# The last experts of a two-block layer: down product of expert 14 moved forward, last up product in staggered column halves, last norm spread over three engines

## The reference, cut to what matters

```python
g, idx = lax.top_k(jnp.swapaxes(aff, 1, 2), cap)        # 16 experts choose 128 tokens each
xs = jax.vmap(lambda hb, ib: hb[ib])(h, idx)
a = jnp.einsum('becd,edf->becf', xs, w_gate)
u = jnp.einsum('becd,edf->becf', xs, w_up)
y = jnp.einsum('becf,efd->becd', jax.nn.silu(a) * u, w_down) * g[..., None]
out = jax.ops.segment_sum(y.reshape(-1, d), flat, num_segments=bsz * n)
...
x = x + gt2 * out
return rmsnorm_2(x, g_final)                            # x * rsqrt(mean(x*x) + eps) * gain
```

## Time and profile before

| what | us |
|---|---|
| median of 3 runs (lowest to highest) | 2581.66 (2574.31 to 2585.56) |
| the profiled execution's own time | 2583.6 |
| its span | 2581.9 |
| PE busy | 2456.7 (95%) |
| DVE busy | 1627.3 (63%) |
| ACT busy | 1058.0 (41%) |
| POOL busy | 211.6 (8%) |

### The profile page before, as it was taken

One profiled execution on the slowest core, in us unless ns is written; L12 is line 12 of the kernel. 1 busy time (PEld: TensorE's weight loads), 2 busy tenths in 40 slices (PEclk: granted clock), 3 DMA queues, 4 the chain that ended last, 5 costly groups with the idle time before them and its releaser, 6 DMA issues.

```text
span 2581.9 us, 30627 instructions
## 1 busy us (share of the span) xinstructions
PE 2456.7 (95%) x11985; PEld 2005.2 (78%) x11985; DVE 1627.3 (63%) x2028; ACT 1058.0 (41%) x1558; POOL 211.6 (8%) x224
## 2 busy tenths in 40 slices
PE   7999889999999999999999999989995999999996
PEld 6787568888888877888787898866684788888884
DVE  6999745225243645444443871477456899999986
ACT  4234434325131221121212522166244677777765
POOL 1000320000000000000000100000103011111100
PEclk9999889999999999999999999999996999999998
DMA  4111021221111322232222311110227899999988
GB/s 149 66 41 45 33 90 68 72 98 34 41 50 44 103 82 99 81 122 81 96 91 71 128 72 34 49 33 18 83 90 269 321 390 391 391 396 392 396 333 298
DMA packets 116412, 370.64 MB, mean 144 GB/s; under 512 B 6309, under 2 KB 15701, under 8 KB 116304
## 3 DMA queue, kind: packets, MB, share of 16 engines
q1 hardware_dynamic: 94832, 293.63, 29.8%
q0 software_dynamic: 21472, 75.51, 9.3%
HBM read 343.89 MB, written 25.26 MB: 143 GB/s over the span
## 4 chain that ended last, share of the span: by engine, by line
PE 83%; DVE 9%; ACT 3%; DMA 2%; issue 2%; POOL 1%; SPq 0%; POOLq 0%; ACTq 0%; DVEq 0%
PE banks L433 24%; PE banks L435 24%; PE banks L434 24%; DVE conv_out L1501 4%; DVE w_lo L427 2%; PE banks L2484 2%; PE banks L533 1%; PE banks L2530 1%; PE banks L2351 1%; PE banks L2330 1%; ACT w_hi L420 1%; DMA expert_w<-in_w_up 1%; PE banks L2499 1%; PE banks L2500 1%; PE banks L2626 1%
## 5 line engine op out<-in xcount | busy, mean ns | idle before, releaser
L2018 DVE TENSOR_TENSOR expert_w_lo<-expert_w,expert_w_hi 128x2048 fp32r<-128x2048 f32 x189 | 427.3, 2286 | 30.3 <-ACT expert_w_hi L1341 28.6
L1341 ACT ACTIVATE expert_w_hi<-expert_w 128x2048 fp32r<-128x2048 f32 x192 | 367.1, 1918 | 153.4 <-PE banks L435 133.1
L433 PE MATMUL banks<-act_hi,w_hi 128*128 128x512 f32 x960 | 376.4, 392 | 7.3 <-DVE w_lo L427 4.1
L434 PE MATMUL banks<-act_lo,w_hi 128*128 128x512 f32 x960 | 374.4, 390 | 0.0
L435 PE MATMUL banks<-act_hi,w_lo 128*128 128x512 f32 x960 | 374.2, 390 | 0.0
L420 ACT ACTIVATE w_hi<-w_raw 128x1024 fp32r<-128x1024 f32 x152 | 156.9, 1060 | 299.1 <-PE banks L435 299.0
L427 DVE TENSOR_TENSOR w_lo<-w_raw,w_hi 128x1024 fp32r<-128x1024 f32 x152 | 181.7, 1223 | 140.4 <-ACT w_hi L420 136.1
L433 PE MATMUL banks<-w_hi,act_hi 128*128 128x512 f32 (+1 forms) x640 | 246.3, 385 | 6.6 <-DVE w_lo L427 3.0
L435 PE MATMUL banks<-w_hi,act_lo 128*128 128x512 f32 (+1 forms) x640 | 243.9, 381 | 0.0
L434 PE MATMUL banks<-w_lo,act_hi 128*128 128x512 f32 (+1 forms) x640 | 243.6, 381 | 0.0
L433 PEld LDWEIGHTS banks<-act_hi,w_hi 128*128 128x128 f32 x960 | 180.7, 188 | 47.9 <-issue 4.2
(11 more groups left out here) (404 smaller groups left out, 4111.1 us busy)
## 6 DMA issues: line engine op xcount, KB each, us to landing
expert_w<-in_w_gate SPq DMA_DIRECT2D x32, 2048.0 KB, 10.8
expert_w<-in_w_up SPq DMA_DIRECT2D x32, 2048.0 KB, 11.1
expert_w<-in_w_down SPq DMA_DIRECT2D x32, 2048.0 KB, 10.8
ada_w<-in_w_ada POOLq DMA_DIRECT2D x48, 512.0 KB, 4.1
w_raw<-in_mlp_up_w SPq DMA_DIRECT2D x16, 1024.0 KB, 5.3
w_raw<-in_mlp_down_w SPq DMA_DIRECT2D x16, 1024.0 KB, 5.0
w_raw<-in_w_in SPq DMA_DIRECT2D x10, 1024.0 KB, 5.3
w_raw<-in_w_in SPq DMA_DIRECT2D x18, 512.0 KB, 6.0
```

The source lines that it names most:

```text
L433: nc.tensor.matmul(o_, lh, rh, start=start, stop=False)
L434: nc.tensor.matmul(o_, lh, rl, start=False, stop=False)
L1341: act.activation(EWH[ring][:, 2 * j:2 * j + 2, :], EW[slot][:, 2 * j:2 * j + 2, :], ACT.Copy).then_inc(w_hi, 1)
L2018: dve.tensor_tensor(EWL[slot][:, c, :], EW[slot][:, c, :], EWH[ring][:, c, :], ALU.subtract).then_inc(w_ready, 1)
```

## The change

- The turn of expert 14 leaves the loop. PE's transposes of expert 14's hidden rows stand in the middle of down 13, and down 14 follows right behind down 13; gate 15 comes after it. Second hidden buffers (`HTH2`, `HTL2`) hold expert 14's.
- Slots: down 14 goes to 2 and 3, up 15 to 4 and 5, down 15 to 2 and 3. Their order in SP's queue is down 14, up 15, down 15, behind gate 15.
- Up 15 runs by pieces in staggered column halves, so that half 0 ends one piece and a half before half 1; the transposes of its first half stand before the last piece of half 1, those of its second half within down 15.
- `expert_y` of expert 14 runs on DVE behind the low part of piece N15+8, and its scatter follows.
- `XB` moves to slots 0 and 1 (also waits for the end of gate 15). ACT copies the gain row to PSUM (`PAIR[2]`). DVE norms tiles 0 to 4 with the gain read from there; POOL multiplies tiles 5, 6 and 7 by gain and then by scale. ACT squares the last rows by halves and scales one half of them, DVE the other.

```diff
         def first_piece(e):
             return 8 + 12 * (e - 1)
...
+        POOL_TILES = (5, 6, 7)
...
             for half in range(2):
-                load_expert(LASTE - 1, 2, half, used=N14 + 8 + 2 * half + 2)
+                load_expert(LASTE - 1, 2, half, used=N14 + 4 + 2 * half + 2, slot=2 + half)
             for half in range(2):
-                load_expert(LASTE, 1, half, used=N14 + 4 + 2 * half + 2)
+                load_expert(LASTE, 1, half, used=N14 + 8 + 2 * half + 2, slot=4 + half)
             for half in range(2):
-                load_expert(LASTE, 2, half, used=N15 + 2 * half + 2, slot=half)
+                load_expert(LASTE, 2, half, used=N15 + 2 * half + 2, slot=2 + half)
+            sp.wait_ge(ex_p, N15 + 8)
             sp.wait_ge(y_out, 16 * (NE - 1))
             for t in range(NT):
                 sp.dma_start(XB[:, t, :], acc_d[tok(t), :]).then_inc(BULK[t], 16)
-            for t in range(NT):
-                sp.wait_ge(pl_x, 8 + t + 1)
+            for t in (0, 1, 2, 3, 5, 4, 6, 7):
+                if t in POOL_TILES:
+                    sp.wait_ge(fp_x, POOL_TILES.index(t) + 1)
+                else:
+                    sp.wait_ge(pl_x, 8 + t + 1)
                 sp.dma_start(out[0, tok(t), :], XB[:, t, :]).then_inc(fin_out, 16)
...
+            pool.wait_ge(w_ready, W_SPLIT + N15 + 16)
...
+            def final_gain(t):
+                pool.tensor_tensor(XB[:, t, :], XB[:, t, :], GF[:, :], ALU.mult).then_inc(fp_g, 1)
...
+            def final_scale(t):
+                pool.wait_ge(fp_g, POOL_TILES.index(t) + 1)
+                pool.wait_ge(fz_scale, TILES_SCALE)
+                pool.tensor_scalar(XB[:, t, :], XB[:, t, :], RS[:, 52 + t:53 + t], None, ALU.mult).then_inc(fp_x, 1)
...
+            pool.wait_ge(pl_sq, 8 + POOL_TILES[0] + 1)
+            final_gain(5)
...
+            for t in POOL_TILES:
+                final_scale(t)
...
@@ ACT @@
+            w_piece_hi(N14 + 11, 5, 1, 0, LASTE - 2)
+            expert_rows_hi(LASTE)
+            w_piece_hi(N15, 2, 0, 1, LASTE)
+            w_piece_hi(N15 + 1, 2, 1, 1, LASTE)
+            expert_hidden_hi(LASTE - 1, HTH2)
+            w_piece_hi(N15 + 2, 3, 0, 2, LASTE)
...
+            w_piece_hi(N15 + 13, 2, 1, 1, NE)
+            act.wait_ge(ex_p, N15 + 8)
+            act.wait_ge(ex_he, LASTE)
+            act.activation(SG[:, :], PAIR[2][:, :], ACT.Silu).then_inc(ex_sg, 1)
             act.activation(SD[:, 63:64], EPSC[:, 0:1], ACT.Sqrt)
...
+            act.activation(PAIR[2][:, :], GF[:, :], ACT.Copy).then_inc(fz_act, 1)
+            w_piece_hi(N15 + 14, 3, 0, 2, NE)
...
+            final_stats(0)
+            w_piece_hi(N15 + 15, 3, 1, 2, NE)
+            final_stats(1)
+            last_hidden_hi(0)
+            final_stats(2)
+            last_hidden_hi(1)
+            for t in range(3, NT):
+                final_stats(t)
+            last_square(0)
+            last_square(1)
...
@@ DVE @@
+            w_piece_lo(N15 + 2, 3, 0, 2)
+            expert_y(LASTE - 1, N14 + 12)
+            w_piece_lo(N15 + 3, 3, 1, 2)
...
+            w_piece_lo(N15 + 8, 4, 0, 2)
+            dve.wait_ge(ex_p, N15 + 4)
+            dve.wait_ge(y_out, 16 * (LASTE - 1))
+            dve.scalar_tensor_tensor(out=YE[:, :], in0=PAIR[0][:, :], scalar=GV[:, LASTE - 1:LASTE], in1=GT2[:, :], op0=ALU.mult,
+                                     op1=ALU.mult).then_inc(ex_y, 1)
+            w_piece_lo(N15 + 9, 4, 1, 2)
...
+            w_piece_lo(N15 + 14, 3, 0, 2)
...
+            def final_rows(t):
+                dve.wait_ge(pl_sd, 8 + t + 1)
+                dlink(dve.reciprocal(RS[:, 52 + t:53 + t], SD[:, 52 + t:53 + t]))
+                dve.scalar_tensor_tensor(out=XB[:, t, :], in0=XB[:, t, :], scalar=RS[:, 52 + t:53 + t], in1=PAIR[2][:, :],
+                                         op0=ALU.mult, op1=ALU.mult).then_inc(pl_x, 1)
...
+            last_hidden(0)
+            last_hidden_lo(0)
+            last_hidden(1)
+            w_piece_lo(N15 + 15, 3, 1, 2)
+            last_hidden_lo(1)
+            dve.wait_ge(fz_act, GAIN_IN_BANKS)
+            final_rows(0)
+            final_rows(1)
+            dve.wait_ge(xs_in, 16 * NE + 16)
+            last_rows(0)
+            final_rows(2)
+            final_rows(3)
+            dve.wait_ge(pl_sd, 8 + NT)
+            dve.reciprocal(RS[:, 57:60], SD[:, 57:60]).then_inc(fz_scale, 1)
...
+            last_rows(1)
+            final_rows(4)
+            dve.wait_ge(fz_act, LAST_RMS)
+            dve.reciprocal(RS[:, 60:61], SD[:, 60:61]).then_inc(fz_scale, 1)
...
@@ PE @@
+            split_product(2, 4, (2, 0), N14 + 8, HTH, HTL, range(4))
+            hidden_T(LASTE - 1, NE)
+            split_product(2, 4, (2, 0), N14 + 8, HTH, HTL, range(4, 8))
...
+            split_product(0, 2, (1, 2), N15, HTH2, HTL2)
+            pe.wait_ge(ex_y, LASTE)
+            split_product(2, 0, (0, 1), N15 + 4)
...
+            for half, piece in ((0, 0), (0, 1), (1, 0), (0, 2), (1, 1), (0, 3), (1, 2)):
+                last_up(half, piece)
+            last_hidden_T(0)
+            last_up(1, 3)
+            pe.wait_ge(ex_y, NE)
+            pe.wait_ge(ex_hl, NE)
+            last_down(0, 0)
+            last_hidden_T(1)
+            last_down(0, 1)
+            pe.wait_ge(ex_hl, NE + 1)
+            last_down(0, 2)
+            last_down(0, 3)
+            for piece in range(4):
+                last_down(1, piece)
```

More of the change, by code:

```diff
@@ L776, in _ @@
                     load_expert(e - 1, 2, half, used=12 * (e - 2) + (16 + 2 * half + 2))
-            N14 = first_piece(LASTE - 1)
             for half in range(2):
@@ L1398, in _ @@
             expert_act(1, first=True)
-            with act.Fori(2, NE - 1) as e:
+            with act.Fori(2, NE - 2) as e:
                 expert_act(e)
[L1401 to L1407, removed]
@@ L1408, in _ @@
-            expert_silu(LASTE, N15 + 4)
-            act.activation(SD[:, 63:64], EPSC[:, 0:1], ACT.Sqrt)
[L1410 to L1416, removed]
+            w_piece_hi(N14 + 4, 2, 0, 0, LASTE - 1)
+            w_piece_hi(N14 + 5, 2, 1, 0, LASTE - 1)
@@ new lines, in _ @@
+            expert_hidden_hi(LASTE - 1, HTH2)
+            w_piece_hi(N15 + 2, 3, 0, 2, LASTE)
+            w_piece_hi(N15 + 3, 3, 1, 2, LASTE)
+            w_piece_hi(N15 + 4, 0, 0, 0, LASTE)
+            w_piece_hi(N15 + 5, 0, 1, 0, LASTE)
+            w_piece_hi(N15 + 6, 1, 0, 1, LASTE)
+            w_piece_hi(N15 + 7, 1, 1, 1, LASTE)
+            w_piece_hi(N15 + 8, 4, 0, 2, LASTE - 1)
+            w_piece_hi(N15 + 9, 4, 1, 2, LASTE - 1)
+            w_piece_hi(N15 + 10, 5, 0, 0, LASTE - 1)
@@ L1417, in _, with final_stats, last_hidden_hi @@
+            w_piece_hi(N15 + 14, 3, 0, 2, NE)
+            def final_stats(t):
+                act.wait_ge(BULK[t], BULK_COUNT[t])
+                plain_stats(8 + t, XB[:, t, :], JB)
+            def last_hidden_hi(half):
                 act.wait_ge(ex_ht, LASTE + half + 1)
@@ L1419, in _, with last_square @@
                                ACT.Copy).then_inc(ex_hc, 1)
[L1421 to L1425, removed]
+            def last_square(half):
+                cols = slice(512 * half, 512 * (half + 1))
+                act.wait_ge(ex_y, NE + half + 1)
+                act.activation(JZ[:, cols], XZ[:, cols], ACT.Square, accum_out=SS[:, 60 + half:61 + half]).then_inc(fz_sq, 1)
+            final_stats(0)
[8 more added lines that the diff above has]
+            last_square(1)
+            act.wait_ge(fz_sq, 2)
+            act.wait_ge(fz_scale, HALF_MEAN)
+            act.activation(SD[:, 60:61], SS[:, 61:62], ACT.Sqrt, bias=SS[:, 62:63], scale=1.0 / D).then_inc(fz_act, 1)
+            act.wait_ge(fz_scale, LAST_SCALE)
+            act.activation(XZ[:, 0:512], YE[:, 0:512], ACT.Copy, scale=RS[:, 60:61]).then_inc(fz_act, 1)
         @block.vector
@@ L2121, in last_hidden, with last_hidden_lo @@
                 dve.tensor_tensor(HE[:, c], SG[:, c], PAIR[1][:, c], ALU.mult).then_inc(ex_he, 1)
-            last_hidden(0)
-            w_piece_lo(N15 + 13, 0, 1, 1)
-            w_piece_lo(N15 + 14, 1, 0, 2)
-            last_hidden(1)
-            for half in range(2):
+            def last_hidden_lo(half):
                 dve.wait_ge(ex_hc, LASTE + half + 1)
@@ L2139, in last_rows @@
                 dve.wait_ge(ex_d, half + 1)
-                dlink(dve.scalar_tensor_tensor(out=YE[:, cols], in0=PAIR[2][:, cols], scalar=GVC[:, 0:1], in1=GT2[:, cols],
+                dlink(dve.scalar_tensor_tensor(out=PAIR[1][:, cols], in0=BK[half], scalar=GV[:, LASTE:NE], in1=GT2[:, cols],
                                                op0=ALU.mult, op1=ALU.mult))
-                dve.tensor_tensor(XZ[:, cols], XZ[:, cols], YE[:, cols], ALU.add).then_inc(ex_y, 1)
-            for t in range(3):
-                plain_rows(8 + t, XB[:, t, :])
+                dve.tensor_tensor(XZ[:, cols], XZ[:, cols], PAIR[1][:, cols], ALU.add).then_inc(ex_y, 1)
@@ L2156, in _ @@
```

(6 more changed lines are left out.)

148 lines of the change are left out of this document (93 added, 55 removed).

## The result

The changed kernel takes 2592.28 us in the median of 7 runs (2590.27 to 2594.94) against 2581.66 before (seven runs as well, 2574.31 to 2585.56). The ratio is 1.0043, 95% interval 1.0034 to 1.0052: slower by 11 us. The forecast was 2578.6, the range 2570 to 2586. The profiled execution has a span of 2592.1 us. The first 2497 us are as before, so the comparison can be made by positions, less about 1.5 us (the turn of the loop in question happens to begin that much earlier here).

What follows compares the result with a forecast made beforehand. TensorE was taken as the bound, busy 2456.7 of 2581.9 us. The last store issued 2.8 us earlier and landing 0.3 quicker gave 3.1 us less than the 2581.66 median: 2578.6 us, range 2570 to 2586.

Steps and rivals of the forecast that it cites:

- The load order: Loads behind gate 15: requests near 2493.5 and 2499, the 10 us pause gone, ScalarE 2.7 us late once.
- The middle by engine: Down 14 to up 15: engine times summed piece by piece, low parts in time up to N15+11, expert 14's output at 2529.1.
- Second stall: Ahead of the last down product: scatter lands in 8.0 us, TensorE waits 2.3 us for the hidden low part behind ScalarE's squares.
- the scale pass: GpSimd's one-input multiply of tiles 5 to 7 in the tail: 1.2 us each, bounds 0.95 and 2.35.
- The gain pass: GpSimd's two-input multiply of tiles 5 to 7 in the tail: 2.35 us each, by a straight line between other sizes.
- The landing: Last store, from issue to landing: 4.2 us, against 4.5 before and 3.9 at the least.
- Rival A: Tail: GpSimd held up in its passes over tiles 5 to 7, span 2584 to 2588, +2.5 to +6; chance 0.20.
- Rival C: End of kernel: scatter lands after 10.8 us, the stats wait longer, no change in the end, span 2581 to 2583; chance 0.14.

Runs made afterwards that it cites:

- e7: The kernel before with the two loads of up 15 put ahead of those of down 14 in SyncE's queue; 2580.97 us, ratio 0.9999.
- e1: The changed kernel with VectorE waiting, behind expert 14's output, until GpSimd has made that expert's scatter; 2583.24 us, ratio 1.0007.
- e2: The changed kernel with two unused VectorE multiplications, one input in PSUM, between expert 14's output and the next low part; 2582.85 us, ratio 1.0003.
- e11: The changed kernel with expert 14's output one piece later on VectorE, four subtractions following instead of five; 2592.09 us, ratio 1.0043.
- e12: The changed kernel with expert 14's output two pieces later on VectorE, three subtractions following; 2591.95 us, ratio 1.0047.
- e5: The changed kernel with a one-column copy on VectorE behind each low part of pieces N15+9 to N15+12; 2582.6 us over 10 runs, ratio 1.0006.
- e6: e1 with GpSimd's three scale passes in three forms: scale column, constant 0.5, two-input multiply by a repeated column; 2584.51 us, one time.
- e3: The changed kernel with ScalarE's last high part and both last hidden copies ahead of all eight tile squares; 2588.57 us, ratio 1.0025.
- e4: The changed kernel with the norm of tiles 5 to 7 back on VectorE, GpSimd without its six passes; 2591.72 us, ratio 1.0044.
- e10: The changed kernel with e5's copies, ScalarE scaling tiles 5 and 6, VectorE norming tile 7, urgent ScalarE copies ahead of squares; 2574.53 us, ratio 0.9975.

## Why the prediction was wrong

- **The load order** was right in its times, within 1.2 us: requests at 2492 and 2498, no pause, ScalarE 3.9 us late for the first half of down 14 (2.7 summed), 0.45 for the second, and never again. What it is worth by itself isn't known: e7 fills the pause with up 15 alone and gets 1.5 us of TensorE's time, with down 14 as late as before.
- **The middle by engine** held: TensorE waited 0.75 us at down 14 and not at all in gate 15 and up 15, 0.60 us at the transposes (1 us summed). VectorE's output of expert 14 ended at 2528.79 (2529.1 summed), 1.2 us late if counted from the turn.
- **The step that failed** is "Second stall": the scatter was priced at 8.0 us from issue to landing, with 10.8 as the upper bound. It took 16.6 (2529.07 to 2545.72), 12.16 of them in its making; the rest, from the making's end to the landing, was 4.5, as before (4.6). The rows of before had that making at 3.35 to 3.40 us in all scatters but one, and the prediction took it as fixed inside the 8.0; it never asked what VectorE did beside it. By e1, e2, e11 and e12 the extra time is the rest of VectorE's run of two-input subtractions. The old order had two in a row behind an output, the new one has five behind that of expert 14. A long run alone isn't enough: behind the output of expert 13 six follow each other, and its scatter was made in 3.35 us.
- **What the delay cost.** Tiles requested 8.4 us later than summed; TensorE's wait of 2.3 us became 11.5. That the place of the squares in ScalarE's queue makes TensorE wait for a tile's landing was in the prediction; its size followed from the scatter. TensorE had been idle from 2545.1; at its restart at 2556.59 the granted clock stood at 0.5 (1.2 GHz), and matmuls came at 0.43 us instead of 0.23. From there to its end it took 14.1 us, where e5 took 11.9 for the same work at the full clock: 2.1 us more.
- **The second term that was mis-sized** is the scale pass: 2.84 us, where 1.2 was taken and 0.95 to 2.35 given as bounds. Three passes, 4.9 us. The upper bound was a two-input pass, on the belief that one input less can't be dearer; e6 shows that it can. The gain pass was right (2.39 measured, 2.35 summed).
- **The landing** of the last store came after 2.65 us instead of 4.2 with the DMA engines quiet, 1.5 us for the kernel.
- Together: GpSimd's passes began 10.2 us late (2565.3, not 2555.1), +4.9 for the scale passes, -1.5 for the landing: 13.6 us, against 2592.1 - 2578.8 = 13.3. (These are positions as they stand; the changed kernel's turn begins 1.5 us earlier than in the trace that the sum was made from, so counted from the turn the passes began 11.7 us late.)
- **The rivals.** Rival A named GpSimd held up by VectorE, but in its passes over tiles 5 to 7. There it isn't so: the gain passes took 2.35 to 2.41 us beside a VectorE that reads the gain from PSUM, as the prediction argued. It was looking at the wrong instruction of GpSimd. Rival C had the sign of the late scatter and a third of its size.
- The Trainium skill (SBUF — State Buffer, § Who interferes with whom) states that a VectorE instruction with two SBUF inputs contends with a GpSimd one that reads SBUF. Taken to the start of the scatter's making, this is what e1, e2, e11 and e12 show. The same section infers that the making of descriptors isn't held up by such a two-input operation, since it needs the write side; here it was held up for up to 10.6 us (12.16 against 1.55), and the measurement decides. The one-input rule of the Trainium skill (GPSIMD Engine Reference, § 4.1, one-input operations at roughly line rate) fails for the multiply by a scalar: 2.76 us with a constant, against 2.39 for the two-input pass.

Open: why GpSimd gets in at the first boundary in one case (the scatter of 13 before six unbroken subtractions; e3's profile) and at none in another (the scatter of 14, e4, e11, e12), with the same 0.35 us between the start of the first subtraction and its own. In the four profiles where it was held, VectorE came to the output from six or more subtractions without a pause; in the scatters that met an unbroken run and got in at its first boundary, it had a wait or a copy of one column just before the output (e3: a wait of 0.23 us). That is what the traces have in common; no run tests it.

## What to carry to other kernels

When an order is packed so that VectorE has no pauses left, look for what GpSimd makes beside it: a scatter or gather whose making was short in every row of before may have been short because VectorE paused, read PSUM or changed its instruction soon. Here the square that waited 10.58 us for its tile held up the copies behind it in ScalarE's queue, and through them TensorE for 11.5 us. Copies that another engine waits for belong ahead of work that waits for a transfer, but only as far as the tail can spare what they push back (e3, e10). And price an operation on GpSimd by a row of the same form, not by its number of inputs.

## What the runs showed of the hardware

- The making of an indirect write of 128 rows takes 1.55 us beside an idle VectorE or one that reads an input from PSUM, 3.35 when a 2.28 us two-input subtraction from SBUF has just begun, and 7.75, 9.96 and 12.16 ahead of three, four and five of them. Ahead of six it took 3.35 as well (the scatter of 13, and e3).
- Such a subtraction delays the start of the making and not the making: 1.4 to 1.5 us of it run beside the next subtraction (before, 2539.30).
- The making of a gather of 128 rows takes 0.98 us, also beside a VectorE instruction with one input in PSUM and its output in SBUF, and 2.77 when a two-input subtraction from SBUF has just begun (e1).
- One copy of a single column between subtractions sufficed to keep it at 3.35 us in the profile and all ten times of e5 below 2587.
- GpSimd on 128x1024 float32: two inputs 2.39 us, scalar from a column 2.85, constant scalar 2.76, two inputs of which one is a repeated column 1.88.
- After 11.5 us of waiting TensorE restarted at a granted clock of 0.5 (1.2 GHz). The stretch from 2545 to 2557 shows 0.64 and the one from 2557 to 2570 shows 0.82 (the clock is the third column from the right):

```profile
2545.00:2557.00 12.00, 0.50 (x2) 0.44 (x2) 1.20 (x2) 6.26 (x11) 0.99 (x1) 0.64 0.87 332
2557.00:2570.30 13.30, 13.30 (x52) 10.75 (x51) 10.54 (x16) 8.46 (x19) 4.97 (x3) 0.82 0.43 173
```
